# Doubling products of both scan directions issued together in four array quarters, attention scores by head pairs, copies and masks moved between engines

## The reference, cut to what matters

```python
def wkv_scan(state0, r, kk, v, decay, b, k, reverse):
    def step(S, inp):
        r_t, kk_t, v_t, w_t, b_t, k_t = inp
        sa = jnp.einsum('bhij,bhj->bhi', S, kk_t)
        S = S * w_t[:, :, None, :] - sa[..., None] * b_t[:, :, None, :] + v_t[..., None] * k_t[:, :, None, :]
        return S, jnp.einsum('bhij,bhj->bhi', S, r_t)
    return lax.scan(step, state0, (r, kk, v, decay, b, k), reverse=reverse)
...
    for d, reverse in enumerate((False, True)):
        ctx_state, y_c = wkv_scan(state0, *c_common, *c_dirs[d], reverse=reverse)
        _, y_l = wkv_scan(ctx_state, *l_common, *l_dirs[d], reverse=reverse)
...
    s = jnp.concatenate([s_win.reshape(B, NA_H, rows, GRID_W, n_win), s_ctx], axis=-1)
    p = jax.nn.softmax(s, axis=-1)
```

## Time and profile before

| | before |
|---|---|
| median of 3 runs | 2142.56 us (2142.12 to 2144.69) |
| the profiled execution's own time | 2142.36 us |
| its span, first to last instruction | 2140.6 us |
| PE busy | 1955.3 us (91%) |
| DVE busy | 1408.8 us (66%) |
| ACT busy | 1042.2 us (49%) |
| POOL busy | 390.9 us (18%) |

### The profile page before, as it was taken

One profiled execution on the slowest core, in us unless ns is written; L12 is line 12 of the kernel. 1 busy time (PEld: TensorE's weight loads), 2 busy tenths in 40 slices (PEclk: granted clock), 3 DMA queues, 4 the chain that ended last, 5 costly groups with the idle time before them and its releaser, 6 DMA issues.

```text
span 2140.6 us, 40342 instructions
## 1 busy us (share of the span) xinstructions
PE 1955.3 (91%) x15183; PEld 1738.9 (81%) x15183; DVE 1408.8 (66%) x2268; ACT 1042.2 (49%) x2078; POOL 390.9 (18%) x330
## 2 busy tenths in 40 slices
PE   6998899978889998998889769999999999999996
PEld 6875788868878887997667669899899998777775
DVE  5545578766867676235544558888799986666665
ACT  4343434446845344333444334444677775555554
POOL 2101000000100000000000003787666670000000
PEclk9999999999999999997999979999999999999998
DMA  7542566653465785331000553555554445556553
GB/s 268 183 173 87 197 206 228 234 198 121 156 217 177 258 273 176 128 114 13 2 3 7 153 120 93 153 161 161 155 142 142 141 139 177 188 193 187 188 192 129
DMA packets 212576, 333.54 MB, mean 156 GB/s; under 512 B 23494, under 2 KB 140860, under 8 KB 212424
## 3 DMA queue, kind: packets, MB, share of 16 engines
q1 hardware_dynamic: 208888, 320.06, 47.1%
q0 software_dynamic: 3536, 11.34, 1.6%
HBM read 330.26 MB, written 1.08 MB: 155 GB/s over the span
## 4 chain that ended last, share of the span: by engine, by line
PE 69%; DVE 13%; DMA 4%; ACT 4%; issue 4%; PEld 2%; SPq 2%; PEldq 0%; POOL 0%; DVEq 0%; ACTq 0%
PE psum L2328 20%; PE psum L2329 19%; PE psum L2330 19%; PE psum L2931 3%; DVE u_turned L2231 2%; DMA u_rows<-in_peer_u_dram 2%; DVE weights_lo L1571 2%; SPq L942 1%; PE psum L2766 1%; PE psum L2755 1%; ACT weights_hi L1090 1%; PE psum L2760 1%; PE psum L2638 1%; PEld psum L2328 1%; PEld psum L2329 1%
## 5 line engine op out<-in xcount | busy, mean ns | idle before, releaser
L1571 DVE TENSOR_TENSOR weights_lo<-weights,weights_hi 128x1024 fp32r<-128x1024 f32 (+2 forms) x336 | 345.5, 1086 | 273.4 <-ACT weights_hi L1090 268.5
L2328 PE MATMUL psum<-input_hi,weights_hi 128*128 128x256 f32 x1288 | 371.9, 289 | 14.1 <-DVE input_lo L1598 5.1
L1090 ACT ACTIVATE weights_hi<-weights 128x1024 fp32r<-128x1024 f32 (+2 forms) x336 | 289.2, 931 | 178.7 <-PEq L2375 117.9
L1069 POOL TENSOR_TENSOR u_lo<-u_turned,u_hi 128x512 fp32r<-128x512 f32 x256 | 330.6, 1314 | 214.8 <-ACT u_hi L1468 214.7
L2329 PE MATMUL psum<-input_lo,weights_hi 128*128 128x256 f32 x1288 | 367.7, 285 | 0.0
L2330 PE MATMUL psum<-input_hi,weights_lo 128*128 128x256 f32 x1288 | 367.2, 285 | 0.0
L2328 PE MATMUL psum<-input_hi,u_hi 128*128 128x256 f32 x1024 | 298.3, 291 | 13.1 <-POOL u_lo L1069 12.1
L2329 PE MATMUL psum<-input_lo,u_hi 128*128 128x256 f32 x1024 | 291.6, 285 | 0.0
L2330 PE MATMUL psum<-input_hi,u_lo 128*128 128x256 f32 x1024 | 291.5, 285 | 0.0
L2328 PEld LDWEIGHTS psum<-input_hi,weights_hi 128*128 128x128 f32 x1288 | 250.6, 195 | 29.6 <-issue 27.8
L2329 PEld LDWEIGHTS psum<-input_lo,weights_hi 128*128 128x128 f32 x1288 | 250.8, 195 | 0.0
(11 more groups left out here) (386 smaller groups left out, 3660.2 us busy)
## 6 DMA issues: line engine op xcount, KB each, us to landing
u_rows<-in_peer_u_dram SPq DMA_DIRECT2D x512, 128.0 KB, 2.6
weights<-in_ffn_w_in_dram SPq DMA_DIRECT2D x44, 1024.0 KB, 7.3
v_rows_even<-in_peer_v_dram SPq DMA_DIRECT2D x64, 512.0 KB, 3.5
v_rows_odd<-in_peer_v_dram SPq DMA_DIRECT2D x64, 512.0 KB, 3.5
weights<-in_ret_w_in_dram SPq DMA_DIRECT2D x24, 1024.0 KB, 7.4
ada_rows_in<-in_ada_w_dram SPq DMA_DIRECT2D x24, 1024.0 KB, 5.2
weights<-in_ffn_w_out_dram SPq DMA_DIRECT2D x44, 512.0 KB, 6.3
weights<-in_lru_w_in_dram SPq DMA_DIRECT2D x12, 1024.0 KB, 6.4
```

The costliest lines, as they stand in the source:

```text
L1069: nc.gpsimd.tensor_tensor(UTL[:, b, half, :], turned[:, half, :], UTH[:, b, half, :].bitcast(F32), ALU.subtract).then_inc(s_ul[b], 1)
L1090: nc.scalar.activation(whi[:, r, at_], wraw[:, r, at_], ACT.Copy).then_inc(s_whi[r], 1)
L1571: ins = nc.vector.tensor_tensor(wlo[:, r, at_], wraw[:, r, at_], whi[:, r, at_].bitcast(F32), ALU.subtract)
L2328: nc.tensor.matmul(o, ah, bh, start=start, stop=False)
```

## The change

- **Locked items.** t, y and xy (`LOCKED`) are issued for both directions at once, where direction 1's item stands. For each j the order is direction 0 in its two quarters, then direction 1 in the two others (direction 1's t and y write to the crossed half of the partitions, and its xy reads from there and writes back). The item waits for what both directions need.
- **Head pairs.** ns is issued for two heads in one place (that of the even head); their two L2638 products come first, in the two row halves and two banks, then the two L2640. nm and nx of both heads follow, at the even head's place; nt and no stay where they were.
- **no** is written as twice as many products of 64 output partitions each, in turn in the two column halves.
- **mixed_plan** holds attention and other work back until the next item that isn't the second of a pair, and sorts nm and nx behind the other attention items.
- **Copies.** ScalarE copies t and y of direction 0 alone; VectorE copies those of direction 1 (`tensor_copy`, 128x256 from PSUM).
- **Masks.** GpSimd makes a_level for both directions (12 of a block), VectorE none. The first two of a direction wait for a_raw of that direction, the later ones for the copy of y of two levels before.

```diff
+LOCKED = ("t", "y", "xy")
...
-            beside.setdefault(NA_FIRST + NA_APART * i + later, []).append((what, i))
+            at_ = NA_FIRST + NA_APART * (i if what in ("nt", "no") else i // 2 * 2) + later
+            beside.setdefault(at_, []).append((what, i))
...
+    waiting = []
     for at_, item in enumerate(rwkv_plan()):
-        for what, i in sorted(beside.get(at_, []), key=lambda x: x[1]):
-            yield None, None, None, what, i
...
+        waiting += sorted(beside.get(at_, []), key=lambda x: (x[0] in ("nm", "nx"), x[1])) + [OTHER_WORK[x] for x in (at_,) if x in OTHER_WORK]
+        _, d, _, what, n = item
+        if not (what in LOCKED and d == 1 or what in PAIRED and n == 1):
+            yield from ((None, None, None, *w) for w in waiting)
+            waiting = []
         yield item
...
+                def level(n):
+                    nc.gpsimd.tensor_tensor(AM[d][:, n % 2].rearrange("p a b c -> p (a b) c"), flat(AA[d]),
+                                            SQM[:, 8 * d + n, :].unsqueeze(1).broadcast_to([P, 4, 64]), ALU.mult)\
+                        .then_inc(s_am, 1)
+
+                if what == "lev":
+                    pool.wait_ge(s_aa, 4 * k + 2 * d + 2)
+                    pool.wait_ge(s_rel, 2 * k + d + 1)
+                    for m in range(2):
+                        level(m)
+                elif what == "t" and n < 5:
+                    evacuated(U("y", n - 1) if n > 1 else U("lev"))
+                    level(n + 1)
...
-                elif what == "t":
+                elif what == "t" and d == 0:
                     out_of(u, TI[d][:, :, :, :].rearrange("p a b c -> p (a b c)"), src=first(256))
-                elif what == "y":
+                elif what == "y" and d == 0:
...
-                    for m in range(2):
-                        level(m)
...
-                elif what == "t" and n < 5:
-                    if n == 1:
-                        evacuated(U(k, d, "lev"))
-                    level(n + 1)
+                elif what in ("t", "y") and d == 1:
+                    b = take(u)
+                    nc.vector.tensor_copy(flat((TI if what == "t" else YY)[d]), squares_(b)).then_inc(s_free[b], 1)
...
+                banks = [free_bank(na_unit("ns", i + x)) for x in range(2)]
...
+                for x in range(2):
+                    half = slice(64 * x, 64 * x + 64)
+                    nc.tensor.matmul(PS[:, banks[x], :], NQ[half, h // 2, qt * P:(qt + 1) * P], NK[half, h // 2, :],
+                                     start=True, stop=False, skip_group_check=True)
+                for x in range(2):
+                    nc.tensor.matmul(PS[:, banks[x], S:2 * S], FLIP[:, :], BIAS[:, qt, h + x, :], start=False, stop=True,
+                                     skip_group_check=True).then_inc(s_full[banks[x]], 1)
...
+                    for c in range(2):
+                        ins = nc.tensor.matmul(PS[64 * c:64 * c + 64, 7, h * 64:(h + 1) * 64],
+                                               NPT[:, i % 2, j * P + 64 * c:j * P + 64 * c + 64], NV[:, j, h * 64:(h + 1) * 64],
...
+                if what in LOCKED:
+                    of_both = lambda what, n: [UNITS["rwkv"] + RW_UNIT[k, e, what, n] for e in range(2)]
+                    banks = [free_bank(v) for v in of_both(what, n)]
+                    if what == "t":
+                        for v in (of_both("xy", n - 1) if n > 1 else of_both("lev", 0)):
+                            evacuated(v)
+                    elif what == "y":
+                        pe.wait_ge(s_am, 12 * k + (4 if n == 1 else 2 * n + 2))
+                    else:
+                        for v in of_both("t", n) + of_both("y", n):
+                            evacuated(v)
+                    for j in range(4):
+                        for e in range(2):
+                            for c in range(2):
+                                here, there = slice(64 * c, 64 * c + 64), slice(64 * (c ^ e), 64 * (c ^ e) + 64)
+                                if what == "t":
+                                    left, right, to = XX[e][here, j // 2, j % 2, :], SQM[here, 16, :], there
...
+                                ins = nc.tensor.matmul(PS[to, banks[e], j * 64:j * 64 + 64], left, right, start=True, stop=True)
+                                if (j, c) == (3, 1):
+                                    ins.then_inc(s_full[banks[e]], 1)
```

53 lines of the change are left out of this document (18 added, 35 removed).

## The result

The changed kernel takes **2134.4 us** (median of 5, 2130.8 to 2135.3) where the kernel before took 2144.7 beside it; the ratio is 0.995, with a 95% interval of 0.9939 to 0.9962. It is 10 us faster. I had said 19 us (2123), so the sign and the range held and the size did not: about half of the forecast gain came. The profiled execution took 2135.3 us, with a span of 2133.2.

The account below looks back on a forecast made before the run. The prediction took TensorE, busy 91% of the span, as the bound, giving way to waits for copies and subtractions. Levels −10.8 us and edges −8.2 summed to −19.0, so 2123 us, with an 8 in 10 range of 2108 to 2143.

Parts of the forecast that it names:

- Less work on PE, and PE no longer the bound: 975 to 1195 us: 42 us come off PE; 2100 us if PE stayed the bound, which it would not.
- the walk: Levels of four blocks: chain of products, copies and subtractions followed item by item, summing to 96.6 us against 107.4.
- The plain level of 3.67 us: Levels: from one t to the next 3.67 us, PE working 1.9 of it; twenty such levels 73.4 us.
- Head pairs inside the levels, +14.8: Four pairs inside the levels make y wait for both exponentials: +3.5 or +3.9 us each, together +14.8 us.
- VectorE's own work, +3.3: Levels of blocks 0 and 1: bm ahead of a subtraction +1.4 us, cv and rg +1.9 us.
- half clock: Start of block 0's levels: TensorE at half clock adds +1.8 us.
- the clock falls: Rival, chance 0.11: half-busy levels run at 1.2 GHz, +34 us in the levels, about 2157 us if it lasts.
- The edges, −8.2: Outside the levels: paired heads, shorter no, no a_level wait, less the first t's longer wait, −8.2 us in all.
- the pairs' −5.6: Block edges: eight single heads at 3.0 us become four pairs at 4.6 us, −5.6 us.
- The wait for a_level: At lev, block edges: TensorE's wait of 2.7 us for a_level goes, since GpSimd starts once a_raw is there.
- Masks on GpSimd hidden: Levels: two masks take GpSimd 1.5 to 3.3 us, within a level's 3.67 and needed one level later, so hidden.
- the levels' 10.8 us: Levels of the four blocks: 96.6 us against 107.4, a gain of 10.8 us.

Follow-up runs that it names:

- warm_small: The changed kernel plus 36 products whose result nobody reads, one behind each y item and each xy item of levels 1 to 4: 2126.5 us.
- singles: The changed kernel with attention by single heads again instead of head pairs, lock step and the rest kept: 2142.2 us.
- unlocked_singles: unlocked with attention by single heads instead of head pairs: 2123.1 us.
- before_masks_gpsimd: The kernel before with only the masks of the levels moved from VectorE to GpSimd: 2143.0 us.
- unlocked_diagonal: unlocked with both directions on the same two quarters of TensorE, the diagonal, as in the kernel before: 2121.6 us.
- unlocked: The changed kernel with t, y and xy issued for each direction by itself, each with its own direction's waits, instead of in lock step: 2120.9 us.
- attention_only: The kernel before with head pairs, halved output products, the change's order and corrected wait at ab; quarters, copies and masks as before, no lock step: 2124.0 us.
- unlocked_side_out: unlocked with VectorE's other work (bias product, convolution and bonus steps) moved out of the levels: 2118.4 us.
- masks_on_vector: The changed kernel with the masks of the levels on VectorE again, none on GpSimd: 2133.5 us.
- side_out: The changed kernel with VectorE's other work (bias product, convolution and bonus steps) moved out of the levels: 2124.3 us.

## Why the prediction was right in sign and wrong in size

- **Less work on PE, and PE no longer the bound: right.** It was 27.5 us less busy in the levels, items of 0.69 us, a pair's two score products 1.06 us from start to start of the next group, no of sixteen 0.69 us for 1.10. Of 42 us some 10 reached the end of the kernel; the walk had said 19.
- **The plain level of 3.67 us: 0.23 too long.** Two subtractions took 0.75 us, not 0.89, and VectorE's copy 0.42 to 0.43, as taken.
- **Head pairs inside the levels, +14.8: about right as far as xy.** From xy's release of PE (1057.05) the next xy came at 1063.40, 6.35 us for the walked 6.55; block 3's at 5.7 for 5.8.
- **VectorE's own work, +3.3: too small.** Block 1's first level took 1048.50 − 1042.01 = 6.5 us, 3.1 over a plain one, where I had 1.9 for cv and rg and 0.75 for the no ahead of y. I had not reckoned that GpSimd's masks would slow them (below).
- **The step that failed: the term "half clock" of the levels' sum, put at +1.8, with "the clock falls" apart from it as a rival at 0.11.** In the change 38 of the levels' 106 us ran at 1.2 GHz, against 5 of 107 before. By the rival's own price (34 us if it lasts through the levels) that is an estimate of 12 us where the sum had 1.8. What a run measured is less: warm_small, with the levels' clock at 1.00, 1.00, 0.93 and 1.00, got 8 us back, 4.8 in the levels and 3.8 at the edges, its fillers' cost taken off. So the clock owns about half or more of the 9.5 us missing in the levels. I had treated as an alternative what was a consequence of the forecast: my own walk left TensorE 1.9 us of work in 3.67 and waits of up to 2 us, and the earlier trace rows showed what can follow such a stretch. A share of it belonged in the sum. That the clock decides the sign only from half of the levels on was a fair threshold, and it hid that a third of them costs a large part of the gain.
- **The rest of the gap in the levels** is in part two stops of TensorE (3.2 us, last section) and the first level of block 1; the walk's error in the other direction (0.23 us a plain level) makes what is left larger. No run closes this sum.
- **The edges, −8.2: measured −8.0, and not for these reasons alone.** Of its terms the pairs' −5.6 is borne out: without pairs the edges are 7.4 us longer in lock step (singles) and 8.2 out of it (unlocked_singles), some of it at 1.2 GHz. (The kernel as a whole loses only 2 us by single heads out of lock step, since its levels are 2.1 us shorter then.) The wait for a_level did go, but before_masks_gpsimd gets 1.5 us for it, not 2.7. The index at ab, which I had not costed, measured 6.7 us as a whole, and whole outputs lengthen the edges by 8.2 us where I had 1.5. The parts add up to far more than 8.0, so something that I hadn't costed took it back; that the total fits is luck.
- **Masks on GpSimd hidden: right**; TensorE never waited for them.
- **The rule on PSUM evacuation.** The Trainium skill (TensorEngine Tiling (Array Packing), Performance Considerations) says that tiling speeds up TensorE "but not PSUM evacuation", and the trace agrees as far as it goes: by occupancy alone the time was to be 2100 and it was 2134.4, with waits for copies and subtractions of 0.66 and 0.92 us in every plain level. unlocked_diagonal, with the two quarters of before, is as fast as unlocked with four.
- **Not asked at all:** whether the parts separately do better. "Locked, every item waits for both" stood in the prediction, yet the levels' 10.8 us hung on it. Against unlocked it costs 13.5.

What stays open: if the parts simply add, attention_only's 21.8 us are 3.5 (order) and 6.7 (wait), and 11.6 for halved outputs and head pairs together. How these divide outside lock step wasn't run; unlocked_singles says that pairs are at most a small part, which would leave the halves more than the 16 x 0.41 us that their items show. That the parts add isn't shown either: the clock differed between all these runs.

## What to carry to other kernels

When a change makes the bounding engine faster than its consumers, walk the chain, but then ask of the walk itself how busy that engine is and what the trace shows its clock to do at such a share: that cost belongs in the sum. Two independent chains that share engines were better staggered than merged here: merging them put every wait on both and doubled the buffers that an item must find free at one time. So before merging, walk the staggered order too. And cost every line of a diff: one index in a wait measured 6.7 us (4 to 9), and the 60 merged items lost.

## What was new about the hardware

**The clock fell after some stands of 2 us and not after others.** Of five waits of over 2 us in the change's levels three were followed by 1.2 GHz within 4 us (those that end at 1045.98, 1062.05 and 1106.56 us), with 0.74 to 1.34 us of work in the next 2; after two (1012.72, 1152.92) it stayed at 1.00 for the next 4, with 1.08 us of work in the first 2 of them. In warm_small the 2.18 us stand of block 1 is still there, and the clock stayed at 1.00 behind it; behind that of block 2 it fell. So one unread product each in gaps of 0.66 and 0.92 us raised the clock on the whole (from 38 to 3 us at 1.2 GHz in the levels), but which stand costs it can't be told from these traces.

**VectorE and GpSimd held each other up, whoever came second.** Both from the change's trace, block 0 level 3 and block 1 level 1:

```profile
1002.60 2.28 DVE L2011 TENSOR_TENSOR na_bias<-na_bias,na_columns 128x2048 f32<-128x2048 f32 x1
1002.66 2.81 POOL L1070 TENSOR_TENSOR a_level<-a_raw,masks 128x256 f32<-128x256 f32 x1 [2.78 <-ACT a_x L1353]
...
1044.49 0.72 POOL L1070 TENSOR_TENSOR a_level<-a_raw,masks 128x256 f32<-128x256 f32 x1 [1.83 <-ACT a_x L1353]
1044.54 0.96 DVE L1971 TENSOR_TENSOR sc_z<-sc_z 128x256 f32<-128x256 f32 x1
```

A mask of 0.72 us took 2.81 behind the start of VectorE's 2.28; VectorE's product (0.42 us in the kernel before, at 1043.29) took 0.96 behind the start of a mask. In the first the mask came second, in the second VectorE did. The Trainium skill (SBUF — State Buffer, Who interferes with whom) has it that the order of issue decides which one blocks, and the trace agrees. In the prediction I had read only the half of it that harms GpSimd.

**TensorE stopped in the midst of an item**, between products that have no wait of their own:

```profile
1016.16 0.59 PE L2748 MATMUL psum<-a_x,inv 64*64 64x64 f32 x25
1018.30 0.34 PE L2748 MATMUL psum<-a_x,inv 64*64 64x64 f32 x7 [1.56 <-issue]
```

The other such stop in the levels was 1.64 us long, before 1162.02 us. After each of the two the clock fell to 1.2 GHz within 2 us, so they cost more than their 3.2 us. Other runs have such a stop in block 3's levels too (unlocked 1.62 us, unlocked_side_out 1.89, masks_on_vector 0.82), side_out has none. The profile names no releaser, and the DMA view has no packet at all while the first one lasted (1016.7 to 1018.3 us), which doesn't speak for the fetch of instructions. No run here was made to find the cause.
